# Identity products in TensorE's waits, modulation rows spread over 128 rows, the filter root between transform units, and a wait moved behind a branch

## The reference, cut to what matters

```python
for layer in range(DEPTH):                       # first block
    u = rms_norm(h, norm_mix[layer])
    mix = even_mixer(...) if layer % 2 == 0 else odd_mixer(...)
    # even: HGRN2 recurrence and forgetting ("fox") attention; odd: differential attention
    h = h + mix
    h = h + hierarchical_moe(rms_norm(h, norm_ffn[layer]), ...)   # 32 experts, 2 of 8 in 1 of 4 groups
for i in range(DEPTH):                           # second block
    m_l = (silu_c @ w_mod[i] + b_mod[i])[:, None, :]              # one row of 6 x 1024
    sh1, sc1, g1, sh2, sc2, g2 = jnp.split(m_l, N_MOD, axis=-1)
    hl = modulate(x, norm1_g[i], sh1, sc1)       # rmsnorm(x) * (1 + scale) + shift
    ol = attention_mixer(...) if i % 2 == 0 else hyena_mixer(...)
    x = x + g1 * ol
    x = x + g2 * sq_relu_mlp(modulate(x, norm2_g[i], sh2, sc2), mlp_w1[i], mlp_w2[i])
# in hyena_mixer, the long filters of two orders n:
h = h * lax.rsqrt(jnp.sum(h * h, axis=(0, 1), keepdims=True) + EPS)
K = jnp.fft.rfft(kfull, n=2 * L, axis=0)         # done as products with transform tables
```

## Time and profile before

| | |
|---|---|
| time of 3 runs (us) | 2453.2 median, 2452.45 to 2458.16 |
| the profiled execution (us) | 2461.33, of it 2459.5 span and 1.83 around it |
| mean granted clock of PE over the span | 0.972 |
| busy share: PE, DVE, ACT | 95%, 76%, 55% |
| instructions of `keep_running` | 208, that is 104 products |

### The profile page before, as it was taken

The page is one execution under the profiler, slowest core; times in us unless marked ns, Lnnn a source line. Parts: engine busy times, 40 slices in busy tenths (PEclk is TensorE's granted clock), DMA queues, the critical chain, the costliest instruction groups (busy, mean ns, idle before and its releaser), DMA issues.

```text
span 2459.5 us, 30043 instructions
## 1 busy us (share of the span) xinstructions
PE 2344.1 (95%) x11222; PEld 1737.9 (71%) x11222; DVE 1876.0 (76%) x2192; ACT 1356.9 (55%) x1499; POOL 20.3 (1%) x39
## 2 busy tenths in 40 slices
PE   7999999999998979999999998999999999999998
PEld 6566877777775466777777776556588865845987
DVE  3746999999997554999999998887467755664665
ACT  3234988888886142888888886136433312102332
POOL 0000000000000000000000000000000000000000
PEclk9989999999999988999999999999999999998999
DMA  9213989988897311898889988653165842532460
GB/s 345 107 69 135 376 361 373 383 361 361 361 373 280 139 67 69 350 384 360 362 361 373 382 362 321 211 188 125 49 226 217 299 139 101 200 142 77 181 230 18
DMA packets 115418, 603.67 MB, mean 245 GB/s; under 512 B 5209, under 2 KB 8353, under 8 KB 90557
## 3 DMA queue, kind: packets, MB, share of 16 engines
q1 hardware_dynamic: 111536, 588.83, 61.5%
q0 software_dynamic: 3792, 13.62, 1.6%
HBM read 601.38 MB, written 1.05 MB: 245 GB/s over the span
## 4 chain that ended last, share of the span: by engine, by line
PE 57%; DVE 18%; issue 13%; ACT 9%; DMA 2%; DVEq 1%; SPq 0%; ACTq 0%
PE bank L968 12%; DVE slab_parts L2702 9%; ACT high L1886 6%; PE bank L1273 4%; PE bank L1602 4%; PE bank L1225 3%; PE bank L1094 3%; PE bank L1252 3%; PE bank L1214 2%; PE bank L1531 2%; PE bank L1533 2%; PE bank L1532 2%; PE bank L1512 2%; PE bank L1514 2%; PE bank L1012 2%
## 5 line engine op out<-in xcount | busy, mean ns | idle before, releaser
L2702 DVE TENSOR_TENSOR slab_parts<-ring,high 128x2048 fp32r<-128x2048 f32 x384 | 862.1, 2287 | 34.0 <-ACT high L1886 31.9
L1886 ACT ACTIVATE high<-ring 128x2048 fp32r<-128x2048 f32 x384 | 728.1, 1916 | 40.1 <-PE bank L1225 32.3
L1225 PE MATMUL bank<-high,xT_parts 128*128 128x512 f32 x1024 | 291.8, 406 | 18.1 <-DVE slab_parts L2702 14.2
L1729 ACT ACTIVATE arena<-bank 128x512 f32<-128x512 f32 (+4 forms) x174 | 95.5, 587 | 384.9 <-PE bank L1602 90.4
L1225 PE MATMUL bank<-slab_parts,xT_parts 128*128 128x512 f32 x1024 | 277.4, 392 | 0.0
L968 PE MATMUL bank<-ring,xT 128*128 128x512 f32 (+3 forms) x576 | 242.6, 583 | 6.7 <-ACT xT L1729 4.0
L1225 PEld LDWEIGHTS bank<-high,xT_parts 128*128 128x128 f32 x1024 | 182.9, 188 | 78.1 <-DVE slab_parts L2702 38.7
L1225 PEld LDWEIGHTS bank<-slab_parts,xT_parts 128*128 128x128 f32 x1024 | 192.4, 188 | 45.0
L1892 ACT ACTIVATE arena<-bank 64x512 f32<-64x512 f32 (+2 forms) x352 | 185.1, 535 | 56.6 <-PE bank L1252 51.3
L968 PEld LDWEIGHTS bank<-ring,xT 128*128 128x128 f32 x576 | 112.1, 196 | 134.4 <-issue 125.8
L2375 DVE TENSOR_TENSOR slab_parts<-ring,high 128x2048 fp32r<-128x2048 f32 x64 | 145.7, 2290 | 60.3 <-ACT high L1749 59.8
(11 more groups left out here) (388 smaller groups left out, 3533.8 us busy)
## 6 DMA issues: line engine op xcount, KB each, us to landing
ring<-in_moe_w_gate SPq DMA_DIRECT2D x64, 2048.0 KB, 8.3
ring<-in_moe_w_up SPq DMA_DIRECT2D x64, 2048.0 KB, 9.3
ring<-in_moe_w_down SPq DMA_DIRECT2D x64, 2048.0 KB, 9.1
ring<-in_mlp_w SPq DMA_DIRECT2D x32, 2048.0 KB, 12.7
ring<-in_w_mod SPq DMA_DIRECT2D x24, 2048.0 KB, 8.0
ring<-in_even_w_in SPq DMA_DIRECT2D x7, 2048.0 KB, 21.2
ring<-in_odd_w_in SPq DMA_DIRECT2D x6, 2048.0 KB, 10.1
ring<-in_h_w_in SPq DMA_DIRECT2D x6, 2048.0 KB, 8.3
```

The lines of the kernel that those rows point to most:

```text
L1225: last = mm(dst[:, :], seated2[:, 4 * half + k, e], part_[:, k, :], start=(half == a == k == 0), stop=(half == a == 1 and k == 3))
L1886: act_fn(hi, weight_half(layer, name, half), ACT.Copy).then_inc(sem(f"high{layer}"), 1)
L2702: v.tensor_tensor(low, w, hi.bitcast(F32), ALU.subtract).then_inc(sem(f"low{layer}"), 1)
```

## The change: what it does

1. `keep_running` gets a column argument and is called in more places. In all 156 identity products are added to the 104: 8 ahead of tile 0 of `turn.mix0`; 2 ahead of the wait for `turn.mix0`'s copies; 2 and 3 at steps 8 and 9 of the fox attention; 4 ahead of `fox_o`; 3 behind `turn.even_out`; in each MoE layer 8 and 2 ahead of the routers of tile 0 and 1, and 9 ahead of the last `down(1, PAIRS, 0)`; 16 ahead of `turn.mix1`; 6 behind `diff_kT`; 6 and 2 at steps 8 and 9 of the differential attention; 26 ahead of `diff_o`; 4 ahead of `c_wide_ready`; 4 and 6 ahead of the tiles of `turn.n1_1`; 16 in place of 12 ahead of tile 1 of `turn.n2_0` and `turn.n2_1`, and 9 behind each.
2. `spread` multiplies over 128 rows: the weights are a column of the whole identity, the table is `routers[:, 0:512]`. DVE zeroes that table (one memset of 128x512) before the rows are loaded into it, and POOL waits for it (`mod_tables_ready`).
3. The filter root's 16 products go in fours behind the first four units of `filter_dft1`. Its three DVE operations go behind `convolve(1)`, `keep` and `multiply_c("mod1.pre2", 0)`. The planner takes its bank later, so that the banks in between shift by one.
4. The wait for `out_drained` at the end of `moe_short` goes; behind the join of the If/Else stands a wait for `moe_done`, which DVE gives after the last sums (L2675).

```diff
@@ constants
-BESIDE_NORM = {"turn.n2_0": (0, 12), "turn.n2_1": (0, 12)}
+BESIDE_NORM = {"turn.mix0": (8, 0), "turn.mix1": (16, 0), "turn.n1_1": (4, 6), "turn.n2_0": (0, 16),
+               "turn.n2_1": (0, 16)}
+BESIDE_COPIES = {"turn.mix0": 2, "turn.even_out": 3, "turn.n2_0": 9, "turn.n2_1": 9, "diff_kT": 6}
+BESIDE_TILE = (8, 2)
+BESIDE_PROBS = {"fox": {8: 2, 9: 3}, "diff": {8: 6, 9: 2}}
+BESIDE_HIDDEN, BESIDE_WIDE, BESIDE_HEADS, BESIDE_SUBLN = 9, 4, 4, 26
@@ PE, helpers
-            def keep_running(bank, times):
+            def keep_running(bank, times, c0=0):
                 for _ in range(times):
-                    nc.tensor.matmul(banks[bank][:, 0:P], ident, ident, start=True, stop=True)
+                    nc.tensor.matmul(banks[bank][:, c0:c0 + P], ident, ident, start=True, stop=True)
-            def turned(name):
+            def turned(name, following=None):
+                if following is not None:
+                    claim(following)
+                    keep_running(following.bank, BESIDE_COPIES[name])
                 for u in U[name]:
                     drained(pe, u)
@@ spread
-                tell(mm(banks[u.bank][:, :], ident[0:MOD_ROWS, n:n + 1].to_broadcast([MOD_ROWS, P]), mod_rows,
-                        start=True, stop=True), u)
+                tell(mm(banks[u.bank][:, :], ident[:, n:n + 1].to_broadcast([P, P]), mod_table, start=True, stop=True), u)
@@ PE, moe
                     turn_tile(f"turn.ffn{layer}", u3, tile, 2 * layer + 1)
-                    for u in U[f"turn.ffn{layer}"][2 * tile:2 * tile + 2]:
-                        drained(pe, u)
                     if tile == 0:
                         claim(router)
                         pe.wait_ge(sem("routers_loaded"), 32)
+                    keep_running(router.bank, BESIDE_TILE[tile], S)
+                    for u in U[f"turn.ffn{layer}"][2 * tile:2 * tile + 2]:
+                        drained(pe, u)
...
                 with pe.Else():
                     moe_dense(layer)
+                pe.wait_ge(sem("moe_done"), layer + 1)
...
-                down(1, PAIRS, 0)
+                down(1, PAIRS, 0, BESIDE_HIDDEN)
                 down(1, PAIRS, 1)
                 turn_weights(PAIRS)
                 scatter(PAIRS, last=True)
-                pe.wait_ge(sem(f"out_drained{layer}"), len(OUT_BANKS))
@@ PE, filter
                     tell(last, u)
+                    if n == 1 and j < 4:
+                        filter_root(j)
@@ DVE
+            link(v.memset(mod_table, 0.0))
             link(v.memset(one_hot, 0.0))
-            tell(v.memset(one_hot[:, MOD_ROWS - 1:MOD_ROWS], 1.0), "one_hot_ready")
+            tell(v.memset(one_hot[:, MOD_ROWS - 1:MOD_ROWS], 1.0), "mod_tables_ready")
```

More of the change, by code:

```diff
@@ L313, in make_plan @@
         if i == 1:
-            p.take("filter_inv")
-        if i == 1:
             p.take("hyena_turn", 2)
@@ L318, in make_plan @@
             p.take("filter_dft0", 8)
+            p.take("filter_inv")
             p.take("filter_dft1", 8)
@@ L669, in build @@
         silu_c = small[:, 464:472]
+        mod_table = routers[:, 0:512]
         mod_rows = routers[0:MOD_ROWS, 0:512]
@@ L1016, in attend @@
                         claim(u)
+                        keep_running(u.bank, BESIDE_PROBS.get(name, {}).get(s, 0))
                         ready(s - 2)
@@ L1144, in _ @@
                               (64, 64, [(1, fx_v[:, 0, s * 64:(s + 1) * 64]), (2, fx_v[:, 1, s * 64:(s + 1) * 64])])])
+            u = U["turn.even_out"][0]
+            claim(u)
+            keep_running(u.bank, BESIDE_HEADS)
             pe.wait_ge(sem("fox_o"), 8)
             turn("turn.even_out", ev_o)
-            turned("turn.even_out")
+            turned("turn.even_out", U["even_out"][0])
             project_tiles("even_out", 0, 1)
@@ L1244, in add_parts, with down @@
                     filled(last, u)
-                def down(e, r, half):
+                def down(e, r, half, beside=0):
+                    u, dst = enter(f"down{e}.{half}", r) if beside else (None, None)
+                    if beside:
+                        keep_running(u.bank, beside)
                     if half == 0:
                         pe.wait_ge(sem(f"hidden{layer}"), r * 2 + 1 - e)
-                    u, dst = enter(f"down{e}.{half}", r)
+                    if not beside:
+                        u, dst = enter(f"down{e}.{half}", r)
                     for a, part_ in enumerate(wait_low(f"down{e}", r, half)):
@@ L1380, in _ @@
                               (P, P, [(1, od_v[:, 0, s * P:(s + 1) * P]), (2, od_v[:, 1, s * P:(s + 1) * P])])])
+            u = U["turn.odd_out"][0]
+            claim(u)
+            keep_running(u.bank, BESIDE_SUBLN)
             for tile in range(NT):
@@ L1394, in _ @@
             moe(1)
+            u = U["of_ctx"][0]
+            claim(u)
+            keep_running(u.bank, BESIDE_WIDE)
             pe.wait_ge(sem("c_wide_ready"), 1)
@@ L1550, in _ @@
             turn("turn.n2_0", u3, 6)
-            turned("turn.n2_0")
+            turned("turn.n2_0", U["mlp0.hidden"][0])
             mlp(0)
@@ L1589, in filter_dft, with filter_root @@
                                   src[:, k * D + half * 512:k * D + (half + 1) * 512], start=(k == 0), stop=(k == 1))
+                    tell(last, u)
+                    if n == 1 and j < 4:
+                        filter_root(j)
+            def filter_root(j):
+                u = U["filter_inv"][0]
+                if j == 0:
+                    claim(u)
+                for i in range(4 * j, 4 * j + 4):
+                    last = mm(banks[u.bank][:, i:i + 1], std_row[:, i * P:(i + 1) * P], ones[0:1, 0:1],
+                              start=True, stop=True)
+                if j == 3:
                     tell(last, u)
@@ L1634, in _ @@
                     drained(pe, half)
-                for ct in range(KD):
-                    last = mm(banks[u.bank][:, n * KD + ct:n * KD + ct + 1], std_row[:, n * D + ct * P:n * D + (ct + 1) * P],
-                              ones[0:1, 0:1], start=True, stop=True)
-            tell(last, u)
             hyena_turn(0)
@@ L1693, in _ @@
             turn("turn.n2_1", u3, 8)
-            turned("turn.n2_1")
+            turned("turn.n2_1", U["mlp1.hidden"][0])
             mlp(1)
@@ L3070, in _ @@
                      "filter_sums")
+            convolve(1)
+            keep(U["mods1"][0])
+            multiply_c("mod1.pre2", 0)
             u = U["filter_inv"][0]
@@ L3077, in _ @@
             link(v.tensor_tensor(conv_b, conv_b, filter_inv, ALU.mult))
-            convolve(1)
-            keep(U["mods1"][0])
-            multiply_c("mod1.pre2", 0)
             convolve(2)
```

9 lines of the change are left out of this document (4 added, 5 removed).

## The result

| | before | changed |
|---|---|---|
| median of 4 runs (us) | 2453.8 (2452.45 to 2458.16) | 2427.15 (2426.56 to 2428.05) |
| profiled execution (us) | 2461.33 | 2426.67 |
| mean granted clock | 0.972 | 0.993 |

The ratio is 0.9889 (95% interval 0.9872 to 0.9905): 26.7 us or 1.1% faster, inside the range of 2409 to 2440 and 4 us above the 2423 forecast. The two profiled executions lie 34.7 us apart, because that of before was 7.5 us above its median.

A forecast was written before the change was run, and what follows sets the result against it. PE, busy 95%, was taken as the bound, its time set by its clock. Savings of 40.9 us, three quarters counted (30.7), less 1.5 cost gave 29; forecast 30 saved, 2423 against the median 2453.2, range 2409 to 2440.

The forecast's parts named there:

- the two causes named: PE's clock falls behind short waits of 0.8 to 2.4 us, and in 24-row products without any wait.
- the seven that were listed: Half-clock us saved: first spread 5.1, second 6.0, fox's end 5.0, differential attention 4.3, second routing 4.0, first routing 2.6, `turn.n1_1` 2.9.
- differential attention's term: Half-clock stretch at 882.5, PE busy 13.6 us: saving at most 4.7 because DVE bounds it, taken as 4.3.
- The other ten stretches: Start, filter root, both MoEs' tails, both MLPs' first products and others: half of 21.5 us, taken as 11 saved.
- I take 1.0 lost: At `turn.mix1`, 16 products behind the branch overrun the norm's release: net 0.5 us lost, or 2.5 at 0.36 each.
- the higher of the two prices: An added identity product costs 0.24 us at full clock, 0.36 where part is at half.
- Three quarters: Share of the 40.9 us summed over all stretches counted as really clearing: 30.7, less 1.5 of cost, 29.
- Rival 2: The clock clears, but DVE's chains, the ring's transfers and norms take the time: 18 us saved, 2435; chance 0.23.
- Rival 1: The clock falls behind long waits only, so only those are cured: 5 to 8 us less 1.5, about 2448; chance 0.06.
- Rival 3: Products overrun their waits and places start late at half clock: price about 15 us, 2465 with a fifth cleared; chance 0.03.

The follow-up runs named there:

- e2_rows24: The changed kernel with both spreads over 24 rows again and without the memset of the table: 2437.92 us, ratio 0.9918.
- e5_long_waits_only: The changed kernel with identity products in the long waits only, none in the short waits of 0.5 to 2.4 us: 2447.51 us, ratio 0.9953.
- experiment 2: The follow-up on short waits, which ran `e5_long_waits_only` against the changed kernel: 2447.51 us.
- e12: The changed kernel plus 3 identity products in the 0.84 us wait at fox's step 2: executions 2423.24 to 2428.92 us, ratio 0.9882.

## Why the prediction was right

- **What bounds the kernel, and the mechanism**: right. The rounds of both MoEs kept their length; the gain is PE's clock. `e2_rows24` and `e5_long_waits_only` take away the two causes named, few rows and short waits. In the medians 10.8 and 20.4 us come back, more than the whole 26.7; in the traces 12.9 and 13.6 of the 34.7. Both causes are shown, their shares only roughly.
- **The terms**: the seven that were listed came whole in the profiled pair. Taken 5.1, 6.0, 5.0, 4.3, 4.0, 2.6, 2.9; measured between the traces 5.4, 6.4, 5.25, 5.0, 4.1, 2.2, 3.6 (the last with a low stretch in the MLP that went away). Together 29.9 against 32. Of the 5.0 in differential attention 0.6 belong to the second copy of `turn.mix1`. That differential attention's term is due to the products is not shown (experiment 2). The memset, taken as 0.5, took 0.49 us, and 0.7 are lost from the last `down` (18.8 ahead) to the memset of the one-hot rows (1536.23 before, 1518.10 changed, 18.1 ahead); `e2_rows24`, which has no such memset, gets the 0.7 back there.
- **"The other ten stretches", 11**: 7.9, or 8.6 without the memset's 0.7. Start 2.7, `diff_o` 2.9, last `down` 2.0 and the two norms 1.5 each came; `turn.n1_0` and the filter root are the shortfall. Faster PE ahead of DVE's modulation sums waits 1.03 and 1.71 us at `turn.n1_0` where it waited 0 and 1.18, and in this execution lost the clock that it had kept: -3.6 with the memset. The root gave 2.3, of which a new half stretch in the inverse transform took 1.4 back.
- **"I take 1.0 lost" at `turn.mix1`**: mis-sized, 5.3. The place and the sign were right, and the branch's end too: put 3.8 us behind the scatter's, measured 3.3 (770.04 to 773.3). What the sum lacked is the second stop of 2.49 us; the branch took 6.9 us where it took about 6 in the six other traces with these products; and the products ran at half: 5.49 us for 29 instructions, the higher of the two prices. The turn came 6.7 us behind its release, for which 2.3 to 4.4 had been worked out. In `e5` and `e12`, without the second stop, it came 2.7 us behind and the place lost 1.6 and 1.8: there the sum holds.
- **"Three quarters"**: the factor was right for the total of the medians and wrong for its reason. In the profiled pair the terms were nearly whole and the pair differs by 34.7; the median before lay 7.5 us under the profiled one, so it had less half clock to give (beside the experiments, executions of before of 2451.2 and 2461.25 us had mean clocks of 0.980 and 0.972). I had the two numbers side by side and corrected for it only by a word. The same paragraph adds up to 29 and then forecasts 30, without a reason.
- **Luck in the number**: all four executions of the result were of the changed kernel's lower time. Run again, its median was 2436.08, 18.2 us under the kernel before beside it: inside the range still, but 13 above the 2423. The prediction had nothing on executions that differ by 10 us.
- **Rival 2** (DVE and others take the time, 2435) came true in small: DVE sets the gather's start now, after a wait of 1.51 us that wasn't there before. **Rival 1** fell by `e5_long_waits_only`. **Rival 3**'s mechanism is what happened at `turn.mix1`, at one place alone; `diff_o`'s 26 products ended 1.62 us early. Its price was added up to "about 15 us" and then used as 20; with 15 the case comes to 2460. The Trainium skill (TensorE: Matmul & The Clock Gate, Why this matters for your kernels) asks that long idle gaps be avoided; these runs show that it isn't enough, since without the products in the short waits the half stretches of 13.7 and 10.2 us were back. The Trainium skill also says (TensorE: Matmul & The Clock Gate, Part 4: PE-mode transpose) that the full clock doesn't engage for transposes; these runs don't agree, 16 of them took 1.91 us.

## What to carry to other kernels

Where PE is the bound and its granted clock falls, look at the waits ahead of each fall, short ones too, and at products that use few rows; fill the first with products that nobody reads, count them so that they end before the release, and give the second all 128 rows of a zeroed table. Don't put such products behind a far branch, where the branch and a second stop decide when they run. After each filling look one stage on, since the faster engine waits there next. Judge by several executions and look at the same place in several traces: the same open wait costs the clock in one execution and not in another, and one kernel can have two times 10 us apart.

## What the runs showed of the hardware that I had not expected

- The same instructions with the same waits run at full in one execution and at half in another (15.3 us busy in both, 106 and 66 instructions; at fox's step 2 in 2 of 12 traces, at `turn.n1_0` in 3 of 6). Once at half, fox's steps, with products over 66 rows and 64 columns and no gaps, stayed there for 20.5 us until the identity products behind them.
- A taken branch over a long arm stops PE for 3.3 to 6.9 us from its start. Before, it started at the end of the last sum and took 3.74. Changed, it started 4.4 us ahead of that (766.4, sum ended 770.76), with weights still streaming, and took 6.9: it ended 2.6 us behind the last sum instead of 3.8. In the seven other traces with the 16 or 4 products it took about 6 us and ended 1.6 behind the last sum. Three instructions further PE stopped again in most traces: for 2.2 to 2.8 us in six of the eight with products there, not at all in `e5` and `e12`; for 1.67 and 0.26 us inside the turn in two of the six without products. That the stops are the fetch of code by DMA is argued from the five transfers of the instruction queues between 766 and 778 us, not shown; that the branch takes longer because weights stream isn't shown either.
- A product over 128 rows costs PE what one over 24 does: instructions of 512 columns start 429 ns apart at full clock with either.
